# Two transformer blocks on one core: setup vectors loaded into all partitions, decay logarithms earlier, expert router in whole fp32

## What is computed

```python
h = rmsnorm(x, norm1_g)
parts = split_cols(h @ w_in)                   # conv q/k/v, then tokens' columns, then gates
qkv = silu(causal_dwconv(parts q, k, v))       # 1536 columns, 4 taps
aq, ak = l2norm(q) * 64**-0.5, l2norm(k)
beta = sigmoid(parts["a_beta"])
g = -exp(a_log) * softplus(parts["a_alpha"] + dt_bias)     # decay logarithms, 8 heads
o_a = gated_delta_rule(aq, ak, av, g, beta)    # chunks of 64, triangular inverse
o_b = attention over 64 keys chosen by an indexer
x = x + (gate_a * (o_a @ w_proj_a) + gate_b * (o_b @ w_proj_b)) @ w_out

xt = rmsnorm(x, norm2_g)                       # mixture of experts
glog = xt @ w_router_group + b                 # 4 groups, top 1
elog = xt @ w_router_expert + b                # 16 experts, top 2 in the group
x = x + sum of chosen experts; then final rmsnorm
# second block: norm, w_in_2 (with 8 forget logits), two mixers, w_out_2, FFN, gated PLE term
```

## Time and profile before

| | |
|---|---|
| median of 3 runs | 924.37 us (923.44 to 927.68) |
| the profiled execution, and its span | 923.62 us, 921.6 us |
| TensorE matmul, busy | 878.9 us, 95% |
| TensorE weight load, busy | 812.8 us, 88% |
| VectorE, busy | 629.1 us, 68% |
| ScalarE, busy | 485.8 us, 53% |
| mean granted clock of TensorE | 0.992 |
| moved by DMA | 156.01 MB, 169 GB/s |

### The profile page before, as it was taken

One profiled execution on the slowest core, in us unless ns is written; L12 is line 12 of the kernel. 1 busy time (PEld: TensorE's weight loads), 2 busy tenths in 40 slices (PEclk: granted clock), 3 DMA queues, 4 the chain that ended last, 5 costly groups with the idle time before them and its releaser, 6 DMA issues.

```text
span 921.6 us, 16498 instructions
## 1 busy us (share of the span) xinstructions
PE 878.9 (95%) x7197; PEld 812.8 (88%) x7197; DVE 629.1 (68%) x762; ACT 485.8 (53%) x585; POOL 44.4 (5%) x66
## 2 busy tenths in 40 slices
PE   5999989998997999999999899989999999999998
PEld 4998889998976999999979788989989999999986
DVE  4977578599747864569885887895466655455564
ACT  5548623467445754457775653655546443443463
POOL 6000060000000000000000000121000000000000
PEclk9999999999998999999999999999999999999999
DMA  7745410232206976469974454241554565555521
GB/s 233 247 143 179 138 49 4 92 138 92 92 0 222 354 292 223 166 244 359 358 235 152 139 181 137 92 165 65 184 167 159 190 210 191 192 183 184 183 92 46
DMA packets 87310, 156.01 MB, mean 169 GB/s; under 512 B 6092, under 2 KB 59717, under 8 KB 83270
## 3 DMA queue, kind: packets, MB, share of 16 engines
q1 hardware_dynamic: 86486, 154.64, 49.4%
q10 hardware_dynamic: 752, 0.33, 0.1%
HBM read 153.90 MB, written 1.05 MB: 168 GB/s over the span
## 4 chain that ended last, share of the span: by engine, by line
PE 79%; DVE 14%; ACT 3%; issue 2%; DMA 0%; POOL 0%; ACTq 0%; DVEq 0%; POOLq 0%
PE ps L1026 9%; PE ps L1029 9%; PE ps L1028 9%; PE ps L1044 7%; PE ps L1045 7%; PE ps L1046 7%; DVE w_lo L1759 5%; PE ps L1464 4%; PE ps L1465 4%; PE ps L1466 4%; PE ps L1242 3%; PE ps L1537 2%; PE ps L1539 2%; PE ps L1538 2%; ACT w_hi L537 2%
## 5 line engine op out<-in xcount | busy, mean ns | idle before, releaser
L1759 DVE TENSOR_TENSOR w_lo<-raw,w_hi 128x2048 fp32r<-128x2048 f32 (+2 forms) x147 | 334.4, 2280 | 142.6 <-ACT w_hi L537 141.4
L537 ACT ACTIVATE w_hi<-raw 128x2048 fp32r<-128x2048 f32 (+2 forms) x147 | 277.6, 1892 | 76.1 <-PE ps L1046 27.5
L1026 PE MATMUL ps<-h_hi,w_hi 128*128 128x256 f32 x768 | 220.0, 287 | 5.5 <-ACT arena L652 1.5
L1028 PE MATMUL ps<-h_lo,w_hi 128*128 128x256 f32 x768 | 218.0, 284 | 0.0
L1029 PE MATMUL ps<-h_hi,w_lo 128*128 128x256 f32 x768 | 218.0, 284 | 0.0
L1026 PEld LDWEIGHTS ps<-h_hi,w_hi 128*128 128x128 f32 x768 | 148.0, 193 | 6.4 <-issue 3.9
L1028 PEld LDWEIGHTS ps<-h_lo,w_hi 128*128 128x128 f32 x768 | 148.0, 193 | 1.7 <-issue 1.4
L1029 PEld LDWEIGHTS ps<-h_hi,w_lo 128*128 128x128 f32 x768 | 148.0, 193 | 0.0
L1044 PE MATMUL ps<-w_hi,h_hi 128*128 128x512 f32 (+1 forms) x240 | 94.6, 394 | 0.5 <-DVE h_lo L2149 0.5
L1045 PE MATMUL ps<-w_lo,h_hi 128*128 128x512 f32 (+1 forms) x240 | 93.3, 389 | 0.0
L1046 PE MATMUL ps<-w_hi,h_lo 128*128 128x512 f32 (+1 forms) x240 | 93.3, 389 | 0.0
(11 more groups left out here) (433 smaller groups left out, 1359.5 us busy)
## 6 DMA issues: line engine op xcount, KB each, us to landing
raw<-in_w_in SPq DMA_DIRECT2D x36, 1024.0 KB, 5.2
raw<-in_w_exp_up SPq DMA_DIRECT2D x16, 1024.0 KB, 5.1
raw<-in_w_exp_down SPq DMA_DIRECT2D x16, 1024.0 KB, 5.0
raw<-in_w_exp_gate SPq DMA_DIRECT2D x15, 1024.0 KB, 5.1
raw<-in_w_ffn_gate SPq DMA_DIRECT2D x11, 1024.0 KB, 5.3
raw<-in_w_ffn_up SPq DMA_DIRECT2D x11, 1024.0 KB, 5.3
raw<-in_w_ffn_down SPq DMA_DIRECT2D x11, 1024.0 KB, 4.9
raw<-in_w_out SPq DMA_DIRECT2D x8, 1024.0 KB, 5.1
```

Source lines behind the costliest of these rows:

```text
L537: act.activation(w_hi[:, j % SPL, 0:kt * n], raw[:, j % RAW, 0:kt * n], ACT.Copy).then_inc(w_high, 1)
L1026: pe.matmul(o, hi[:, k, cols], a_hi[:, k, :], start=(k == 0 and (whole or c == 0)), stop=False)
L1028: pe.matmul(o, hi[:, k, cols], a_lo[:, k, :], start=False, stop=False)
L1759: dve.tensor_tensor(w_lo[:, j % SPL, 0:kt * n], raw[:, j % RAW, 0:kt * n], w_hi[:, j % SPL, 0:kt * n].bitcast(F32), sub).then_inc(w_ready, 1)
```

## The change

Four things are changed. The rows loads move from ACT's queue to SP's, between chunks 0 and 1, and x is loaded in two halves with a semaphore each; rep and the rope frequencies are loaded straight into 128 partitions ahead of the router weights, and the matmuls and copies that repeated them go. VectorE copies chan after it has scaled x. The decay logarithms start ahead of the normalisation of the heads and of a split, with ACT's Exp of a_log first and Sigmoid last. Gate chunk 0 is done in two halves around the turns of q_dec. The router multiplies turned, unsplit x (x_cols, copied from PSUM by VectorE) as the stationary operand with rt_raw in whole fp32; rt_raw is multiplied by norm2_g once, and ACT's h_hi and VectorE's h_lo of that norm go, with the copy and turn of the logits.

```diff
-            sp.dma_start(x_tok[:, :, :], x[0].rearrange("(t p) d -> p t d", p=P)).then_inc(s_x, 16)
+            sp.dma_start(x_tok[:, 0], x[0, 0:P]).then_inc(s_x, 16)
+            sp.dma_start(x_tok[:, 1], x[0, P:2 * P]).then_inc(s_x1, 16)
...
+            def repeated_rows():
+
+                for c, v in ((C_FIN, final_norm_g.unsqueeze(0)), (C_ALOG, a_log), (C_DT, dt_bias),
...
+                    sp.dma_start(rep[:, c:c + n], v.broadcast_to([P, n])).then_inc(s_rep, 16)
+                sp.dma_start(over[:, 0, :], rope_freq.broadcast_to([P, 32])).then_inc(s_rep, 16)
+
             for i, (src, kt, n) in enumerate(chunks):
                 slot = i % RAW
                 if i == 1:
-                    sp.wait_ge(s_rows, 144)
...
-                        sp.dma_start(rep_row[0:1, c:c + v.shape[1]], v).then_inc(s_rep, 16)
-                    sp.dma_start(freq_row[0:1, :], rope_freq).then_inc(s_rep, 16)
+                    setup_rows()
                 if i == RAW:
+                    repeated_rows()
                     sp.dma_start(rt_raw[:, :, 0:4], w_router_group[0].rearrange("(k p) n -> p k n", p=P)).then_inc(s_rt, 16)
...
             act.wait_ge(s_tok_ev, 2)
+            act.wait_ge(s_rep, 176)
+            act.activation(alog, rep[:, C_ALOG:C_ALOG + 8], ACT.Exp).then_inc(s_spm, 1)
+            softplus(0)
             act.activation(beta, z_tok[:, :, Z_BETA:Z_BETA + 8], ACT.Sigmoid).then_inc(s_beta, 1)
-            softplus(0)
-            act.activation(alog, rep[:, C_ALOG:C_ALOG + 8], ACT.Exp).then_inc(s_spm, 1)
...
-            norm(1, 1, R_N2)
+            act.activation(primed, ones[:, 0:1], ACT.Sqrt)
+            for c in range(2):
+                squares(1, c)
+            act.wait_ge(s_ms, 2)
+            act.activation(rms, rms, ACT.Sqrt).then_inc(s_rt_n, 1)
...
-            turn_x(0, repeat_rows)
+            turn_x(0)
...
+            pe.wait_ge(s_tok_ev, N_TOK_BLK)
+            gate_chunk(GATE, 0, s_gate_ev, range(4))
             pe.wait_ge(s_qn, 2)
...
-            pe.wait_ge(s_tok_ev, N_TOK_BLK)
-            gate_chunk(GATE, 0, s_gate_ev)
+            gate_chunk(GATE, 0, s_gate_ev, range(4, 8))
...
+            def router(ks):
+
+                for k in ks:
+                    pe.wait_ge(s_h, 8 + 2 * (k // 2) + 2)
+                    for t in range(NT):
+                        m = pe.matmul(bank(5)[:, 20 * t:20 * t + 20], x_cols[:, k, P * t:P * t + P], rt_raw[:, k, 0:20],
+                                      start=(k == 0 and t == 0), stop=(k == KD - 1 and t == NT - 1))
...
-                pe.wait_ge(s_rt_lo, 1)
-                small_cols(5, slice(0, 20), range(0, 4), 1)
+                pe.wait_ge(s_rt_lo, 2)
+                router(range(0, 4))
                 turn_half(1, 1)
-                small_cols(5, slice(0, 20), range(4, 8), 1)
-                turn_cols(5, 20, 1, s_small_ps)
+                router(range(4, 8))
...
+            def turned_columns(bs):
+
+                for b in bs:
+                    dve.wait_ge(s_xt, 4 + b + 1)
+                    dve.tensor_copy(x_cols[:, 2 * b:2 * b + 2, :],
+                                    split3(bank(TURN_BANK[1][b]), 2)).then_inc(s_h, 2)
...
+            dve.tensor_tensor(rt_raw[:, :, 0:20], rt_raw[:, :, 0:20], last(chan[:, R_N2:R_N2 + 8], 20),
+                              mult).then_inc(s_rt_lo, 1)
...
-            softplus(0, 2)
+            softplus(0, 2, normalized_heads)
             dve.scalar_tensor_tensor(glog, sp1, -1.0, mid(alog, 2), mult, mult).then_inc(s_glog, 1)
+            ahead(TOK[2][0])
...
-            low(1, chan[:, R_N2:R_N2 + 8], (2, 3))
-            dve.wait_ge(s_cols_ps, 1)
-            dve.tensor_copy(cols_t[0:20, :], bank(5)[0:20, 256:512]).then_inc(s_cols, 1)
+            turned_columns((2, 3))
             root_of(1, r_moe)
```

More of the change, by code:

```diff
@@ L230, in two_block_program @@
         junk2 = view(0, NT, DM)
-        rep_row = view(9940, C_ALL)[0:1]
         z_tok = view(0, NT, TOK_W)
@@ L1085, in _ @@
             pe.transpose(bank(7)[:, 0:R_ALL], rows[:, :], ident[0:R_ALL, 0:R_ALL]).then_inc(s_chan_ps, 1)
-            def repeat_rows():
-                pe.wait_ge(s_const, 2)
-                pe.wait_ge(s_rep, 176)
-                for r in range(3):
-                    n = min(512, C_ALL - 512 * r)
-                    m = pe.matmul(bank(4 + r)[:, 0:n], ones[0:1, :], rep_row[0:1, 512 * r:512 * r + n],
-                                  start=True, stop=True)
-                m.then_inc(s_chan_ps, 1)
-                pe.matmul(bank(6)[:, 400:432], ones[0:1, :], freq_row[0:1, :], start=True,
-                          stop=True).then_inc(s_chan_ps, 1)
-            turn_x(0, repeat_rows)
+            turn_x(0)
             for c in range(6):
@@ L1765, in low @@
                 for b in bs:
-                    dve.wait_ge(s_hhi, 8 * turn + 2 * b + 2)
+                    dve.wait_ge(s_hhi, 8 * (turn - (turn > 1)) + 2 * b + 2)
                     for k in (2 * b, 2 * b + 1):
@@ L1829, in final_and_mix @@
                 dve.wait_ge(s_dve, m)
-            dve.wait_ge(s_chan_ps, 1)
-            dve.tensor_copy(chan[:, :], bank(7)[:, 0:R_ALL]).then_inc(s_chan, 1)
-            dve.wait_ge(s_chan, 1)
             first_norm()
             ahead(0)
-            dve.wait_ge(s_chan_ps, 3)
-            for r in range(3):
-                n = min(512, C_ALL - 512 * r)
-                dve.tensor_copy(rep[:, 512 * r:512 * r + n], bank(4 + r)[:, 0:n]).then_inc(s_chan, 1)
-            dve.tensor_copy(over[:, 0, :], bank(6)[:, 400:432]).then_inc(s_chan, 1)
             dve.tensor_tensor(gain_mix, chan[:, R_FIN:R_FIN + 8], chan[:, R_NMIX:R_NMIX + 8], mult)
@@ L1861, in _ @@
             ahead(TOK[0][0])
-            dve.wait_ge(s_chan, 5)
+            dve.wait_ge(s_rep, 176)
             dve.wait_ge(s_pos, 16)
@@ L1901, in _, with normalized_heads @@
             step(dve.tensor_scalar(nrm[:, :, 0:8], nrm[:, :, 0:8], HD ** -0.5, None, mult))
-            for t in range(NT):
-                heads = qkv[:, t, 0:DM].rearrange("p (h d) -> p h d", d=HD)
-                m = mark(dve.tensor_tensor(heads, heads, last(nrm[:, t, :], HD), mult))
-            dve.wait_ge(s_dve, m)
-            ahead(TOK[2][0])
+            def normalized_heads():
+                for t in range(NT):
+                    heads = qkv[:, t, 0:DM].rearrange("p (h d) -> p h d", d=HD)
+                    m = mark(dve.tensor_tensor(heads, heads, last(nrm[:, t, :], HD), mult))
+                dve.wait_ge(s_dve, m)
             dve.wait_ge(s_tok_ev, 2)
@@ L2160, in mix @@
                         ahead(OU[1][1], end)
-                        low(2 * n + 1, chan[:, row:row + 8], (0, 1))
+                        if n == 0:
+                            turned_columns((0, 1))
+                        else:
+                            low(3, chan[:, row:row + 8], (0, 1))
             def p_low():
```

48 lines of the change are left out of this document (28 added, 20 removed).

## The result

The changed kernel took 920.15 us in the median of 7 runs (918.35 to 921.22), and the kernel before on the same chip 924.37 (7 runs, 923.44 to 927.68): a ratio of 0.9949 with a 95% interval of 0.9929 to 0.9968. A repetition gave 920.16 (8 runs) and 0.9940 (0.9915 to 0.9965). The prediction was 916.7, its range 913.5 to 920.7. So the time fell into the range near its end, and the gain was about half of what the sum said.

What follows compares the result with a forecast made beforehand. TensorE was taken as the bound, busy 878.9 of 921.6 us. Terms 4.3 + 2.8 - 0.6 + 1.2 = 7.7 off 923.62 gave 915.9, with the median's 0.75 916.7; range 913.5 to 920.7.

Steps and rivals of the forecast that it cites:

- A: The start: first weight matmul 3.4 us earlier, plus 1.5 for the clock, less 0.6: gain 4.3, bounds 2 and 5.
- the same bytes stand ahead now, so the rows land at 9.1 to 9.4: The start: chunk 0 landed at 9.1 us, so rows behind it on SP's queue follow by 9.4; usable at 8.82 before.
- only pos_i to issue: The start: ACT issues just this load, so its table is loaded by about 3.2 us.
- the Trainium skill's rule: The start: engines take queues in turn, so rows left on ACT's queue would have come at about 8 us.
- the price of the clock at the start: The start: 1.5 us gained as half clock from 18.60 to 22.00 doesn't recur, 0.6 lost to half-clock first matmuls.
- rival (1): Half clock recurs after the start and after glog, -3.0 us, leaving 4.7: 919.7 us; chance 0.12.
- Rival (2): The start: rows land after chunk 1 too, 3 us later, TensorE starts at about 16.8: 919.3 us; chance 0.06.
- Rival (3): SP's repeated-row loads issue slowly, 2.8 us each, and chunk 4 comes late: 13 us slower, 938; chance 0.03.
- B: Decay logarithms: TensorE's 1.34 us wait for glog and the half clock behind it go: gain 2.8, lower bound 1.3.
- C: Gate chunk 0 in halves: TensorE wins 0.8 us while waiting for ACT, ACT's chain loses 0.6: -0.6, bounds -0.8 and 0.
- D: The router: whole-fp32 passes at 0.114 us bring the logits 1.2 us earlier, upper bound 2.1, and the gain carries.
- Rival (4): The router: passes at half clock, 0.23 us each, bring the logits at 280.9, -2.4 us: 920.3; chance 0.07.

Runs made afterwards that it cites:

- A alone: Changed kernel with the decay logarithms, gate chunk 0 and router changes undone, only the start's changes left: 921.96 us median of 12 runs, ratio 0.9966.
- the lower group: Kernel before, unchanged: 33 of 65 runs on all occasions, at 922.6 to 924.7 us; the profile shown ahead of the prediction belongs here.
- the upper one: Kernel before, unchanged, profiled again: 927.81 us, one of the slower executions; 32 of 65 runs took 926.8 to 930.1 us.

## Why the prediction came out as it did

The range held the time, but not for its reasons, and that is luck: of the 7.7 forecast 2.8 came in the profiled execution, and it was the wide range that took this in. Point by point the four terms were 4.3, 2.8, -0.6 and 1.2, and they measured 0.6, 3.0, -0.4 and, at the experts, 0.3; what no term had was +0.9, -1.4 and -0.2.

**A failed.** The step was "the same bytes stand ahead now, so the rows land at 9.1 to 9.4". They were used at 11.96. The chunk ahead of them was itself 1.1 us late through the 256 pieces of pos_i, which the sum had as "only pos_i to issue", a cost of ACT's time and not of the DMA's; and rows came 1.7 behind it. With that went the sentence that the sum is the same by the row's reading and by the Trainium skill's rule: rows on ACT's queue were used at 8.89 (not the 8 named there) and made the first weight matmul 2.1 us earlier. Its start without these two, at 14.5, is what the prediction named 14.2.

The second failed step is the price of the clock at the start, "I take 1.5 and expect it not to recur" less 0.6 for first matmuls at half clock (bounds 0 and 1.7). From the first weight matmul to the first eviction it took 6.02 us at full clock (rows on ACT's queue), 7.52 before and 7.94 in the changed kernel: the 1.5 was right, the 0.6 was 1.9, above its own bound. So it was in three profiles of this start (the changed kernel twice, and with six empty instructions); in four with parts undone behind it half clock didn't lie on the weight matmuls. That is nearest to rival (1), but the clock found no other gap there, it rose later. What the prediction put for rival (1), "a low stretch follows each gap of TensorE so far", was misread: the profile before has none behind the waits of 1.50 us at 138.40, 2.48 at 224.50 and 1.97 at 517.65.

Rival (2) had the start, at 16.8, and not the cause: the rows did not land behind chunk 1, which landed at 14.1. Rival (3) is out: the repeated loads took 0.43 to 0.45 us each to issue and the first, of 512 KB, 3.46, and TensorE waited for no chunk in the first 60 us.

**B held**, wait and clock. That the clock's part belongs to it isn't certain in every execution: with A alone the same gap had no low clock behind it.

**C held in sign** and was 0.36 instead of 0.6.

**D held at the logits** (1.22) and at 0.112 a pass, and failed in "the ranks, the order of the groups, the expert loads and the gather all hang on the logits, so it carries": the ranks lost 1.03 to the low clock, and between the kernels with the new and the split router the medians differ by 0.15. Rival (4), the router's passes at half clock, didn't come; the low clock came behind them.

**What was not in the sum.** From the first expert matmul to the end every kernel with part A takes longer than the kernel before in its two profiles (629.1 to 630.1 us in eleven profiles against 627.9 and 628.2). It is spread over the experts' matmuls of 256 columns: their mean spacing is 118.3 ns in the three profiles without part A and 119.9 in the eleven with it. The matmuls of 256 columns with h_lo in the second block have 119.9 in the kernel before and in the changed one, so it isn't all of TensorE's work. Two rows of one expert from TensorE's timeline of the kernel before, and the two at the same places of the changed one's:

```profile
361.05 0.28 PE L1465 MATMUL ps<-w_lo,arena_rounded 128*128 128x256 f32 x1
...
371.78 0.28 PE L1465 MATMUL ps<-w_lo,arena_rounded 128*128 128x256 f32 x1
```

```profile
357.16 0.28 PE L1478 MATMUL ps<-w_lo,arena_rounded 128*128 128x256 f32 x1
...
368.03 0.28 PE L1478 MATMUL ps<-w_lo,arena_rounded 128*128 128x256 f32 x1
```

They are 10.73 us and 10.87 apart, 1.3% more for the same instructions at full clock. Part A takes freq_row out of SBUF, 128 bytes in each partition, so that what is laid out behind it moves; that this is the cause was not tried.

**The forecast stood on one of two faces of the kernel before.** All durations came from an execution of the lower group. Against the upper one (span 925.8) the same changed kernel is 7.0 us faster, and that half of the executions adds to the measured gain. The matmuls that repeat the rows were costed at 2.8; they cost 2.8 or 5.0.

## What to carry to other kernels

Before costing a move from one queue to another, list every transfer in flight at that time with its number of pieces, whoever issued it: a load of 1 KB in 256 pieces delayed 1 MB by over a microsecond. A stretch at half clock was worth 0.2 to 2 us here by what ran in it, and a gap of TensorE may or may not bring one, so a term for it is a chance and not a sum. Where the gap is known, filler matmuls can take it away: in the one profile with them it was gone, the median won 1.5 us with overlapping intervals, and the clocks of the other executions say that low stretches were left. If the times of a kernel fall in two groups, take a profile of each before predicting.

## What the runs showed of the hardware

TensorE's first instruction came at 8.8 to 12.0 us in all fourteen profiles. The first record of full clock starts at 13.1 to 15.5 in ten of them, and at 20.1 to 23.7 in four: the upper execution of the kernel before, the changed kernel twice, and the one with six empty instructions. So the half clock on chunk 0 in the changed kernel and the slow repeats of the upper execution before are one and the same late rise. Whether the kernel or the single execution decides on it, fourteen profiles don't settle.

The same gap had a low clock behind it in some executions and not in others: 1.3 us at glog with it in four profiles and without it in one, and 1.97 us ahead of TensorE's matmuls in the second block (517.65 before) without it in the first profile of before and with it in the changed kernel at 514.68. The Trainium skill ("TensorE: Matmul & The Clock Gate", section What's actually happening) says that the chip watches TensorE by a clock of its own, which doesn't start with the kernel; these runs agree.

At 515.9 the low stretch cost 0.2 us at most, since TensorE had a wait of 1.07 for VectorE at 526.22 in the profile of before, which is gone in the changed kernel's: the lost time was taken up by that wait. Of the fourteen profiles the four without a low stretch near there have that wait, 1.06 to 1.10 us, and the ten with one don't.
